# Dilated attention in a two-block model step: queries and keys projected by token block, 512 columns a head, turned there and transposed back

## The reference, cut to what matters

```python
def _dilated_mixer(x, w_in, w_out, pos):
    z = x @ w_in                                   # 256 x 1024 @ 1024 x 5120
    q = z[..., :nq] -> 3 groups x 8 heads x 128    # one set of queries per dilation
    k, v -> 8 heads x 128
    q, k = _partial_rotary(q, pos), _partial_rotary(k, pos)
    for g, (span, dilation) in enumerate(DIL_PAIRS):   # dilations 1, 4, 16
        o, l = windowed attention of q[:, g] on k, v, with its logsumexp
    o = sum over g of softmax_g(lses) * outs[g]
    return o @ w_out

def _partial_rotary(x, pos):                       # 128 features a head, rot = 32, half = 16
    x1, x2, rest = x[..., :half], x[..., half:rot], x[..., rot:]
    return concatenate([x1 * cos - x2 * sin, x2 * cos + x1 * sin, rest])
```

## Time and profile before

| | |
|---|---|
| runs | 1770.16, 1769.71, 1764.72 us; median 1769.71 |
| the profiled execution | 1763.27 us, its span 1761.5 us |
| mean granted TensorE clock | 0.987 of full speed |
| PE busy | 1674.8 us (95%) |
| PEld busy | 1537.8 us (87%) |
| DVE busy | 1094.4 us (62%) |
| ACT busy | 928.7 us (53%) |
| POOL busy | 319.2 us (18%) |
| chain that ended last, by engine | PE 79%, DVE 11%, ACT 4%, DMA 3%, issue 3% |

### The profile page before, as it was taken

How to read it: one execution, slowest core, us unless ns; L and a number is a source line. 1 busy time by engine, 2 the same in 40 slices (tenths; PEclk the granted TensorE clock), 3 DMA queues, 4 the chain that set the end, 5 groups by cost and what they waited for, 6 DMA issues and landing times.

```text
span 1761.5 us, 30723 instructions
## 1 busy us (share of the span) xinstructions
PE 1674.8 (95%) x12856; PEld 1537.8 (87%) x12856; DVE 1094.4 (62%) x1760; ACT 928.7 (53%) x1457; POOL 319.2 (18%) x228
## 2 busy tenths in 40 slices
PE   6999999999998999999999998889999899889998
PEld 5889998999888999989998987769988789869986
DVE  4555656787455556458774667567545777776544
ACT  4646755666446477446664554336633454436531
POOL 0000020243000000202330143016500200007400
PEclk9999999999999999999999999999999999999999
DMA  5624345455554233445545532115564433235552
GB/s 201 183 77 155 120 158 189 162 199 180 193 179 132 90 141 123 170 174 192 190 175 189 226 120 73 52 71 194 180 220 174 161 129 144 96 120 215 203 199 77
DMA packets 45546, 274.09 MB, mean 156 GB/s; under 512 B 4704, under 2 KB 8928, under 8 KB 16352
## 3 DMA queue, kind: packets, MB, share of 16 engines
q1 hardware_dynamic: 44688, 267.41, 43.4%
q10 hardware_dynamic: 720, 4.72, 0.7%
HBM read 271.06 MB, written 1.05 MB: 154 GB/s over the span
## 4 chain that ended last, share of the span: by engine, by line
PE 79%; DVE 11%; ACT 4%; DMA 3%; issue 3%; POOL 0%; SPq 0%; DVEq 0%; ACTq 0%; POOLq 0%
PE b_ps L354 14%; PE b_ps L356 14%; PE b_ps L357 14%; PE b_ps L439 9%; PE b_ps L442 8%; PE b_ps L440 8%; DVE b_wlo L311 3%; DMA b_wraw<-in_w 2%; PE b_ps L960 2%; ACT b_S L912 1%; PE b_ps L939 1%; PE b_ps L1834 1%; PE b_ps L782 1%; DVE b_S L860 1%; PE b_ps L1065 1%
## 5 line engine op out<-in xcount | busy, mean ns | idle before, releaser
L311 DVE TENSOR_TENSOR b_wlo<-b_wraw,b_whi 128x2048 fp32r<-128x2048 f32 (+2 forms) x266 | 576.5, 2171 | 196.3 <-PE b_ps L442 130.9
L354 PE MATMUL b_ps<-b_Hh,b_whi 128*128 128x256 f32 x2232 | 647.0, 290 | 8.5 <-ACT b_zrot L790 5.0
L356 PE MATMUL b_ps<-b_Hl,b_whi 128*128 128x256 f32 x2232 | 633.8, 284 | 0.0
L357 PE MATMUL b_ps<-b_Hh,b_wlo 128*128 128x256 f32 x2232 | 633.6, 284 | 0.0
L303 ACT ACTIVATE b_whi<-b_wraw 128x2048 fp32r<-128x2048 f32 (+2 forms) x266 | 470.8, 1772 | 217.4 <-PE b_ps L442 151.6
L354 PEld LDWEIGHTS b_ps<-b_Hh,b_whi 128*128 128x128 f32 x2232 | 430.2, 193 | 18.0 <-issue 6.9
L356 PEld LDWEIGHTS b_ps<-b_Hl,b_whi 128*128 128x128 f32 x2232 | 430.4, 193 | 1.5
L357 PEld LDWEIGHTS b_ps<-b_Hh,b_wlo 128*128 128x128 f32 x2232 | 430.3, 193 | 0.0
L1418 POOL TENSOR_TENSOR b_fl<-b_ab,b_fh 128x256 fp32r<-128x256 f32 x44 | 93.8, 2131 | 224.9 <-ACT b_fh L1391 224.9
L1473 POOL TENSOR_TENSOR b_gl<-b_relu,b_gh 128x256 fp32r<-128x256 f32 x64 | 85.8, 1348 | 130.9 <-ACT b_gh L1454 130.8
L439 PE MATMUL b_ps<-b_whi,b_gh 128*128 128x512 f32 x256 | 99.7, 390 | 0.0
(11 more groups left out here) (353 smaller groups left out, 2683.2 us busy)
## 6 DMA issues: line engine op xcount, KB each, us to landing
b_wraw<-in_w SPq DMA_DIRECT2D x223, 1024.0 KB, 4.8
b_wraw<-in_w SPq DMA_DIRECT2D x39, 512.0 KB, 3.4
b_bias<-in_rpb SPq DMA_DIRECT2D x8, 512.0 KB, 10.2
b_gains<-in_gains ACTq DMA_DIRECT2D x4, 1024.0 KB, 5.1
b_wraw<-in_w SPq DMA_DIRECT2D x2, 768.0 KB, 4.1
b_cA<-in_cA SPq DMA_DIRECT2D x2, 576.0 KB, 7.9
b_X<-in_x SPq DMA_DIRECT2D x2, 512.0 KB, 5.6
out<-b_X SPq DMA_DIRECT2D x4, 256.0 KB, 2.5
```

The lines of the kernel that those rows point to most:

```text
L311: e.tensor_tensor(wlo[u % NLO][:, 0:n], raw[u % NRAW][:, 0:n], hi.bitcast(F32), ALU.subtract).then_inc(up("w_lo", "wlo", u))
L354: e.matmul(out, wh, x.hi[:, kk, :], start=k == 0, stop=False)
L356: e.matmul(out, wh, x.lo[:, kk, :], start=False, stop=False)
L357: ins = e.matmul(out, wl, x.hi[:, kk, :], start=False, stop=last)
```

## The change

Queries and keys of a head become one tile of 512 columns (three queries and the key, 128 each) of a job with four tiles, projected by row blocks, `per_unit=1, kpart=4`: a fill step is now one row block, and there are four a head, (input half, token half) = (0,0), (0,1), (1,0), (1,1). Each tile has two units, both begun at its first step. Each token half is copied by ScalarE to `rows` (`turned_copy_act`), 32 features of each of the four parts are turned in place by VectorE with a table that lies by tokens (`turned_dve`: two products of 64 columns, one of 128, a wait, one sum of 128), TensorE transposes the four parts into one bank (`turned_pe`), and ScalarE spreads the bank to `diQK` (`turned_act`). The first token half's transposes stand at the head's fourth step, the second's behind the next head's first block. ScalarE's part at a head's first step is `ahead_act`, then the spread of the head before. The score scale moves to the masked minimum (`scale` for 1.0, masks with the opposite sign). Banks: 0 and 1 for the blocks, 2 and 7 for the transposes. The values' second job moves behind all heads, by input halves. `due` changes, and GpSimd's passes are released by the first tile's two banks.

```diff
@@ -53,16 +53,26 @@
...
-    def both(ok):
-        m = np.where(ok, 0.0, BIG)
+    def turns(dim, rot, theta):
+        half = rot // 2
+        inv = np.float32(theta) ** (-np.arange(half, dtype=np.float32) / np.float32(half))
+        ang = tok.astype(np.float32)[:, None] * inv.astype(np.float32)[None, :]
+        cs, sn = np.cos(ang), np.sin(ang)
+        by_tok = np.concatenate([cs, cs, -sn, sn], axis=1)
+        return np.concatenate([by_tok[0:P], by_tok[P:T]], axis=1)
+    c["turns2"] = turns(128, 32, 500000.0)
+    def both(ok, far=BIG):
+        m = np.where(ok, 0.0, far)
...
-    c["dil0"] = both((k <= q) & (q - k <= 128))
-    c["dil1"] = both((k <= q) & ((q - k) % 4 == 0))
-    c["dil2"] = both((k <= q) & ((q - k) % 16 == 0))
+    c["dil0"] = both((k <= q) & (q - k <= 128), -BIG)
+    c["dil1"] = both((k <= q) & ((q - k) % 4 == 0), -BIG)
+    c["dil2"] = both((k <= q) & ((q - k) % 16 == 0), -BIG)
...
@@ -80,7 +90,7 @@
...
-CONST_D = ["cos2", "sin2", "perm2", "dil0", "dil1", "dil2"]
+CONST_D = ["turns2", "dil0", "dil1", "dil2"]
...
@@ -818,6 +828,41 @@
...
+    class Turned:
+        def __init__(self, ctx, table, need):
+            self.rows, self.table, self.need, self.parts = sb(ctx, "rot", [P, 2, 512]), table, need, scr[0:2]
+    def turned_copy_act(e, w, tn, job, j, tb, old):
+        if old is not None:
+            w.wait_ge(*at("full", ("back", *old, tb)))
+        row_act(e, w, job, j, tb, tn.rows[:, tb, :])
+    def turned_dve(e, w, tn, job, j, tb):
+        v = tn.rows[:, tb, :].rearrange("p (g c) -> p g c", g=4)
+        t0, t1 = (tn.parts[tb][:, P * i:P * i + P].rearrange("p (g c) -> p g c", g=4) for i in range(2))
+        cs, sn = (tn.table[:, 64 * tb + a:64 * tb + a + 32].unsqueeze(1).broadcast_to([P, 4, 32]) for a in (0, 32))
+        w.wait_ge(*at(*tn.need))
+        w.wait_ge(*at("free", (job.key, j, tb)))
+        e.tensor_tensor(t1[:, :, 0:16], v[:, :, 16:32], sn[:, :, 0:16], ALU.mult)
+        e.tensor_tensor(t1[:, :, 16:32], v[:, :, 0:16], sn[:, :, 16:32], ALU.mult)
+        e.tensor_tensor(t0, v[:, :, 0:32], cs, ALU.mult).then_inc(up("rot_parts", "rot_parts", job.key, j, tb))
+        w.wait_ge(*at("rot_parts", job.key, j, tb))
+        e.tensor_tensor(v[:, :, 0:32], t0, t1, ALU.add).then_inc(up("rot_rows", "rot_rows", job.key, j, tb))
+    def turned_pe(e, w, tn, job, j, tb, ring):
+        bank = banks.take(w, ("back", job.key, j, tb), ring)
+        w.wait_ge(*at("rot_rows", job.key, j, tb))
+        for g in range(4):
+            ins = e.transpose(bank[:, g * P:g * P + P], tn.rows[:, tb, g * P:g * P + P], ident)
+        ins.then_inc(banks.full(("back", job.key, j, tb)))
+    def turned_act(e, w, job, j, tb, dst):
+        key = ("back", job.key, j, tb)
+        w.wait_ge(*at("full", key))
+        e.activation(dst, banks.tile(key)[:, :].rearrange("p (g t) -> p g t", g=4), ACT.Copy).then_inc(banks.free(key))
...
@@ -827,7 +872,7 @@
...
-        return dict(dict(masks=None, tables=[], base=0, sink=None, plus=False), **kw)
+        return dict(dict(masks=None, tables=[], base=0, sink=None, plus=False, scale=1.0), **kw)
...
@@ -857,7 +902,7 @@
...
-                ins = e.tensor_tensor_reduce(S[:, o:o + ww[qb]], bank[:, o:o + ww[qb]], h["masks"][g][qb], 1.0, init, ALU.add, ALU.max if h["plus"] else ALU.min, mn[:, qb:qb + 1])
+                ins = e.tensor_tensor_reduce(S[:, o:o + ww[qb]], bank[:, o:o + ww[qb]], h["masks"][g][qb], h["scale"], init, ALU.add, ALU.max if h["plus"] else ALU.min, mn[:, qb:qb + 1])
...
@@ -2285,30 +2330,30 @@
...
-                self.tn = Turning("dil", s1, CD("cos2"), CD("sin2"), CD("perm2"), ("cDt",), scr[0:2])
-                self.sets = [(sb(s1, "diQ", [P, 12, T]), sb(s1, "diK", [P, 4, T]), sb(s1, "diV", [P, 2, 512])) for _ in range(2)]
+                self.tn = Turned(s1, CD("turns2"), ("cDt",))
+                self.sets = [(sb(s1, "diQK", [P, 4, 4, T]), sb(s1, "diV", [P, 2, 512])) for _ in range(2)]
...
-            self.qk = [Job(f"diqk{hg}", "c_w_in_2", 0, range(8), [np.arange(D * g + P * h, D * g + P * h + P) for h in range(4 * hg, 4 * hg + 4) for g in range(4)],
-                           H, together=hg == 0) for hg in range(2)]
+            self.qk = [Job(f"diqk{hg}", "c_w_in_2", 0, range(8), [np.concatenate([np.arange(D * g + P * h, D * g + P * h + P) for g in range(4)]) for h in range(4 * hg, 4 * hg + 4)],
+                           H, per_unit=1, kpart=4) for hg in range(2)]
...
-                Q, K, V = self.sets[hg]
-
-                def qk(e, ps, g, Q=Q, K=K, h=h):
-                    e.matmul(ps[:, 0:P], Q[:, 3 * h + g, 0:P], K[:, h, 0:P], start=True, stop=True)
-                    return e.matmul(ps[:, P:P + T], Q[:, 3 * h + g, P:T], K[:, h, :], start=True, stop=True)
+                QK, V = self.sets[hg]
+                def qk(e, ps, g, QK=QK, h=h):
+                    e.matmul(ps[:, 0:P], QK[:, h, g, 0:P], QK[:, h, 3, 0:P], start=True, stop=True)
+                    return e.matmul(ps[:, P:P + T], QK[:, h, g, P:T], QK[:, h, 3, :], start=True, stop=True)
...
-                                  masks=[[CD(f"dil{g}")[:, 0:P], CD(f"dil{g}")[:, T:2 * T]] for g in range(3)], widths=[P, T],
-                                  needs=[("rotated", f"diqk{hg}", 4 * h + 3)], tables=[("cD",)], d=P,
+                                  masks=[[CD(f"dil{g}")[:, 0:P], CD(f"dil{g}")[:, T:2 * T]] for g in range(3)], widths=[P, T], scale=-(128.0 ** -0.5),
+                                  needs=[("free", ("back", f"diqk{hg}", h, tb)) for tb in range(2)], tables=[("cD",)], d=P,
...
-            fill = [("qk", (0, j)) for j in range(16)] + [("qend", (0,)), ("v", (0,)), ("v", (1,))]
-            fill += [("qk", (1, j)) for j in range(16)] + [("qend", (1,))]
-            due = [7, 11, 15, 20, 26, 30, 34, 36]
+            self.blocks = [(pi, tb) for pi in range(2) for tb in range(2)]
+            fill = [("qk", (h, n)) for h in range(8) for n in range(4)] + [("v", (0,)), ("v", (1,))]
+            due = [6, 10, 14, 18, 22, 26, 30, 34]
...
@@ -2325,25 +2370,52 @@
...
-        def place(self, hg):
-            def at_(j):
-                Q, K, _ = self.sets[hg]
-                h, g = j // 4, j % 4
-                return [(Q[:, 3 * h + g, :] if g < 3 else K[:, h, :], 0, P)], -(128.0 ** -0.5) if g < 3 else 1.0, None
-            return at_
+        def qk_pe(self, e, w, h, n):
+            row_pe(e, w, self.qk[h // 4], h % 4, *self.blocks[n])
+            if n == 3:
+                turned_pe(e, w, self.tn, self.qk[h // 4], h % 4, 0, "back")
+            elif n == 0 and h:
+                self.last_pe(e, w, h - 1)
+        def last_pe(self, e, w, h):
+            turned_pe(e, w, self.tn, self.qk[h // 4], h % 4, 1, "back")
+        def copy_act(self, e, w, h, tb):
+            turned_copy_act(e, w, self.tn, self.qk[h // 4], h % 4, tb, None if h == 0 else (self.qk[(h - 1) // 4].key, (h - 1) % 4))
+        def back_act(self, e, w, h, tb):
+            turned_act(e, w, self.qk[h // 4], h % 4, tb, self.sets[h // 4][0][:, h % 4, :, tb * P:tb * P + P])
+        def qk_act(self, e, w, h, n):
+            if n == 0:
+                ahead_act(e, w, self.qk[h // 4], h % 4)
+            if n == 2:
+                self.copy_act(e, w, h, 0)
+            elif n == 3:
+                self.copy_act(e, w, h, 1)
+                self.back_act(e, w, h, 0)
+            elif n == 0 and h:
+                self.back_act(e, w, h - 1, 1)
+        def qk_dve(self, e, w, h, n):
+            if n == 0:
+                ahead_dve(e, w, self.qk[h // 4], h % 4)
+            elif n >= 2:
+                turned_dve(e, w, self.tn, self.qk[h // 4], h % 4, n - 2)
...
-            banks.assign(lin=SOME, att=ATT)
+            banks.assign(lin=[0, 1], back=[2, STAT], att=ATT)
...
-                    rot_pe(e, w, self.qk[i[0]], i[1], self.tn)
+                    self.qk_pe(e, w, *i)
...
-                    for b in row_blocks(self.v[1])[4 * i[0] // 2:4 * i[0] // 2 + 2]:
-                        row_pe(e, w, self.v[1], *b)
-                elif what == "qend":
-                    turn_pe(e, w, self.qk[i[0]], 15, self.tn)
+                    for tb in range(2):
+                        row_pe(e, w, self.v[1], 0, i[0], tb)
+                    if i[0] == 0:
+                        self.last_pe(e, w, 7)
...
@@ -2357,14 +2429,17 @@
...
-            first_rows_act(e, w, self.v[0], self.sets[0][2])
+            first_rows_act(e, w, self.v[0], self.sets[0][1])
...
-                    rot_act(e, w, self.qk[i[0]], i[1], self.tn)
+                    self.qk_act(e, w, *i)
...
-                    tb, = i
-                    ahead_act(e, w, self.v[1], 0)
-                    row_act(e, w, self.v[1], 0, tb, self.sets[1][2][:, tb, :])
+                    if i[0] == 0:
+                        ahead_act(e, w, self.v[1], 0)
+                        self.back_act(e, w, 7, 1)
+                    else:
+                        for tb in range(2):
```

(9 more changed lines are left out.)

## The result

| | before | after |
|---|---|---|
| median of the runs | 1769.93 us (4) | 1791.16 us (4; 1788.80 to 1795.84) |
| ratio | | 1.0138, 95% interval 1.0115 to 1.0161 |
| profiled execution, its span | 1763.27, 1761.5 us | 1795.84, 1793.7 us |
| mean granted clock | 0.987 | 0.975 |

Slower by 1.4%, some 21 to 25 us. The profiled execution is the slowest of the four; that of the kernel before was 6.7 us under its median.

A forecast was written before the change was run, and what follows sets the result against it. TensorE was taken to set the pace. Head 7's scores 13.9 us later, less 3.1 at the end, plus 4 for the clock gave +14.8 on 1763.3, 1778.1; plus 3 toward the median, 1781 us, range 1764 to 1796.

The forecast's parts named there:

- rival 1: Clock falls in every head, as TensorE now waits twice in 19 us: +8, 1789 us in all; chance 0.20.
- TensorE gains 1.4 us a head: Query and key projection on TensorE: four 512-column blocks plus eight transposes, 11.8 us for 13.2, 11 us in all.
- The copy is held: ScalarE's spread copy stands behind a split awaiting block (h, 1); scores start 2.72 us after that block, a new wait.
- The turning comes late: VectorE turns the first token half only after the previous head's probabilities; TensorE's transposes wait 1.6 us, a second new wait.
- 19.05 a head: One head from scores to scores: 2.72 + 9.02 + 7.31 us, against 16.18 before and 14.8 of TensorE's own work.
- The start: First head: turning operations meet GpSimd's passes, transposes start at 1398.0, head 0's scores at 1409.0 (1409.8 before).
- 3.1 us come back at the end: At head 7, values' blocks cover the turning, so the earlier 4.11 us wait and low-clock stretch go; 3.1 us regained.
- I take two falls in six heads: +4: New TensorE waits lower the clock in two of six heads, about 2.0 us each; bounds none and 12.
- the longer wait of rows 11: Argument against the clock falling in every head: of two waits elsewhere, 2.6 and 2.2 us, the longer kept full clock.
- last interval: Interval up to head 7's scores, with four blocks of values in place of a head's two: 21.8 us.

The follow-up runs named there:

- e4: Changed kernel with only the order altered: scores of head h-1 come after the fourth block of head h, not the second; 1750.1 us, 0.9906 of before.
- e2: Changed kernel with ScalarE's spread copy of the head before put in front of the splits ahead; 1769.4 us, 1.0019 of before.
- e3: Changed kernel with each unit's weight split at a step of its own, on both ScalarE and VectorE; 1754.9 us, 0.9939 of before.
- e6: Changed kernel with ten unused constant matmuls filling TensorE's wait before the scores of heads 0 to 6; 1778.9 us, 1.0079 of before.
- e9: Changed kernel with 512 unused columns behind its constants, so later tensors lie in main memory as before the change; 1785.9 us, 1.0113 of before.
- e10: e4 with all four of GpSimd's passes over X moved behind its sum for head 6; 1746.9 us, 0.9895 of the kernel before.
- e7: e4 with GpSimd's four passes over X started only when head 0's second half is transposed back; 1750.0 us, 0.9899 of the kernel before.
- e12: e11 with GpSimd's passes parted: two after head 0's second half is transposed back, two behind its sum for head 6; 1743.0 us, 0.9842 of before.
- e11: e10 with each unit's split at its own step, ScalarE's second one behind the spread of the first half; 1747.8 us, 0.9883 of before.

## Why the prediction was right or wrong

The direction was right, the size too small: 1781 forecast, 1791.2 measured, inside a range that reached to 1796 to take in rival 1. As a change, 14.8 us were worked out on the profiled execution, of which only 11.3 were left against the median of the runs shown; between the medians it is 21.2. The step that failed is the clock, seven falls for two. By its steps:

- **"TensorE gains 1.4 us a head."** Right: where nothing holds TensorE, a head takes 14.82 us (e4) for 16.18.
- **"The copy is held."** Right, in place and size: 2.64 us seven times, for "some 2.5" (2.72 in the sum). e2 takes it away and gets 16 us of stage back. This is the cause of the slowdown: without it (e2) the stage differs from before by 2.6 us.
- **"The turning comes late."** Right: 1.41 us in e3, where it stands alone, for 1.6. In the changed kernel it is 0.3 to 1.3 us; with the full clock throughout (e6) it is 1.34, so it is the slower blocks in front that cover the rest. The four turning operations take 0.22, 0.22, 0.29 and 0.29 us and, overlapping, 0.8 in all, for 1.0.
- **"19.05 a head."** 19.22 without a fall (e9, e6): right from head 3 on. The heads before have no head turn or values yet and took 18.24, 18.26 and 18.57 (e6). The six intervals add up to 112.7 us at the full clock, for 114.3.
- **"The start."** Right to the microsecond: 29.7 us from the first matmul to head 0's scores, for 30.0. Three of the four first operations met a pass and waited for it. TensorE waited 7.85 us, for 8.1. What the prediction didn't see: without any pass 2.8 us of this wait stay, because the copy stands behind a split that waits for its load (e10). Behind the passes it didn't show.
- **"3.1 us come back at the end."** Right: from head 7's scores to the wait of 5.0 us 30.0 us, for 33.2.
- **"I take two falls in six heads: +4."** This step failed. The clock fell in all seven intervals, for 9.9 us (e6), 5.9 more than the sum had. The price of one was too high (1.4 on average for 2.0), their number far too low. It was rival 1, at 0.20: its 1789 came within 2 us, with 12 us for the clock where it was 9.9. The reason against it, the longer wait of rows 11 that did nothing, compared a single wait with a series: here a second wait of 0.3 to 1.3 us and the next 2.64 us follow within 20 us. What decides isn't shown by one wait's length: in e2, waits of 2.84 us alone brought a fall in two of seven heads.
- **The sum and the median.** In the stage: forecast +14.8, measured +18.7. From one to the other: start -0.3, six heads -1.6, last interval +0.1, end -0.1, clock +5.9. The rest of the distance to 1791.2, 6 us, isn't the stage's. 3.6 of it are that I set the kernel before at 1766.3 (its profiled execution and half of the distance to the median), while it measured 1769.9. By subtraction, some 3 us are left for what lies in front of the stage.

**What stays open** are those 3 us. Before the stage, all kernels have the same code. It began at 1377.1 and 1379.0 in two profiles of the kernel before, at 1381.6 to 1393.4 in the other twelve. Part of the scatter is one wait near 60 us, for a projection whose weights load beside the large bias transfers. In the first profile of the changed kernel:

```profile
PE b_ps L1089 <- ACT b_naK L1221: 6.6, 1, 6.6
```

It was 6.6, 5.8, 5.8, 4.5, 4.4, 4.0, 2.5 and 1.8 us in eight of the 14 profiles, under 1 or absent in the others, e4, e7 and both of the kernel before among them. The begin of the stage goes more closely with the clock: in front of it the lower level was granted for 20.4 and 23.8 us in the two profiles of the kernel before, for 27 to 48 us in the other twelve, and for the longest, 47.6 us, in the first profile of the changed kernel. That is a correlation over 14 profiles; no run changed the clock there. And both profiles of the kernel before are of quick executions, 6.7 and 4.8 us under the medians measured beside them, while the first profile of the changed kernel is of the slowest of its four. Two such profiles are too few to say that the change moved anything in front of the stage; e9 put main memory back and didn't settle it.

The Trainium skill (TensorE: Matmul & The Clock Gate, section Back-to-back issue gap) states 131 ns for a sustained 512-column matmul. This kernel doesn't show that: the matmuls of its blocks start every 227 ns, as in rows 4.

## What to carry to other kernels

In an in-order queue, "do it ahead" is an instruction that may wait, and what stands behind it waits too. When a job goes from one to two buffers begun at once, look up which of its waits ends after the next thing that somebody needs from that queue; the cheapest cures are a copy put in front, or the consumer put later (here one line of due times: 41 us). And when waits of a few microseconds come back in each round of a loop, reckon with the lower clock in each round, not in some: 2.64 us with a second wait behind it brought it in six or seven intervals of seven, 2.84 us alone in two, 1.41 us alone in none.

## What the runs showed of the hardware

- The clock: waits of 2.64 us, with one of 0.3 to 1.3 us between them, went with a granted clock of 0.50 (1.2 GHz) for 3.4 us in each head, and for 6.8 us in the first. Against the same intervals of e6 a fall cost 1.2 to 2.0 us in the changed kernel. The price depends on what lies under it: in e9 1.7 us where it began with the scores, on which the chain hangs, 0.8 where it began 1.3 us behind their start. Filling the wait with matmuls that nobody reads made the kernel 10 us faster (e6).
- GpSimd's passes stop VectorE's operations with one SBUF tensor too: the two scalings at 1507.45 in e10 took 4.66 us together and 0.55 elsewhere. I had counted only operations with two. The Trainium skill (SBUF — State Buffer, section SBUF: two separate sides) has VectorE's faster modes in the same lock, and the trace agrees: alone, such a scaling of 256 columns takes 0.35 us, where an operation of 256 columns with two tensors takes 0.43 (rows 7).
- Each waiting operation of VectorE gets through after one pass. Three of the four short ones at the changed kernel's start waited once each, and took 1.5 to 2.4 us for 0.2 to 0.3; a long split (2.29 us) beside passes waited once and took 4.28 (e7). How many operations the passes meet counts, and not only where they stand: two passes in place of four behind head 6 cost TensorE 3.0 us in place of 7.2 (e12, e11).
